# A fused MLA, retention and mixture-of-experts layer on one core: tokens gathered in fp32, four unsplit weight units in 24, a ring of twelve loaded two units at a time

## The reference, cut to what matters

```python
g_sel = argmax(h @ w_group + b_group)                    # one group of 4
e_local = top_k(e_logits[g_sel] + e_bias, 2)             # two of its 8 experts
y = (silu(xb @ w1[e]) * (xb @ w3[e])) @ w2[e]            # 32 experts, w1, w3: 2048x512, w2: 512x2048
out = sum over the 2 chosen experts of e_w * y[token]
h = layer_norm(ALPHA * h + out, ln2_g, ln2_b)
```

## Time and profile before

| what | value |
|---|---|
| median of 3 runs | 2136.24 us (2135.05 to 2139.49) |
| profiled execution, its span | 2134.4 us; the page gives no other time of it |
| PE, PEld, DVE, ACT busy | 97%, 82%, 75%, 60% of the span |
| experts' weights, issues | 380 + 4 of 1024 KB, median 10.4 and 8.1 us to landing |
| read from HBM | 595.05 MB |

### The profile page before, as it was taken

The page is one execution under the profiler, slowest core; times in us unless marked ns, Lnnn a source line. Parts: engine busy times, 40 slices in busy tenths (PEclk is TensorE's granted clock), DMA queues, the critical chain, the costliest instruction groups (busy, mean ns, idle before and its releaser), DMA issues.

```text
span 2134.4 us, 30028 instructions
## 1 busy us (share of the span) xinstructions
PE 2069.4 (97%) x11452; PEld 1749.8 (82%) x11452; DVE 1592.3 (75%) x1450; ACT 1286.2 (60%) x1064; POOL 104.7 (5%) x76
## 2 busy tenths in 40 slices
PE   8999999999999999999999999999999999999986
PEld 8998888899999998887887777777777787777764
DVE  7646664453646375455669999999999999999988
ACT  5445653333333323334347888888888888888883
POOL 1000000000000000001000000000000000000010
PEclk9999999999999999999999999999999999999998
DMA  6554335655454544557777999999999999999996
GB/s 215 159 139 158 118 120 186 208 180 172 146 176 148 166 157 143 192 197 239 233 297 287 399 421 421 421 420 419 418 420 418 421 418 417 417 417 418 417 397 251
DMA packets 168608, 606.48 MB, mean 284 GB/s; under 512 B 20252, under 2 KB 32684, under 8 KB 117452
## 3 DMA queue, kind: packets, MB, share of 16 engines
q1 hardware_dynamic: 164976, 598.01, 73.9%
q0 software_dynamic: 3552, 7.37, 1.1%
HBM read 595.05 MB, written 22.04 MB: 289 GB/s over the span
## 4 chain that ended last, share of the span: by engine, by line
PE 64%; DVE 16%; issue 9%; DMA 7%; ACT 3%; DVEq 0%; POOLq 0%; POOL 0%; SPq 0%; ACTq 0%
PE ps L1991 19%; PE ps L1972 15%; DVE wl L786 11%; DMA raw<-in_w_dram 7%; PE ps L1119 5%; PE ps L1120 5%; PE ps L2349 4%; PE ps L1116 3%; ACT wh L636 2%; PE ps L2104 2%; PE ps L1141 1%; DVE yall L951 1%; PE ps L2064 1%; PE ps L1089 1%; PE ps L2077 1%
## 5 line engine op out<-in xcount | busy, mean ns | idle before, releaser
L786 DVE TENSOR_TENSOR wl<-raw,wh 128x2048 fp32r<-128x2048 f32 x347 | 780.9, 2288 | 39.7 <-ACT wh L636 38.4
L636 ACT ACTIVATE wh<-raw 128x2048 fp32r<-128x2048 f32 x347 | 661.6, 1915 | 132.8 <-DMA raw<-in_w_dram 72.6
L1548 DVE TENSOR_TENSOR wl<-raw,wh 128x2048 fp32r<-128x2048 f32 (+1 forms) x168 | 379.8, 2263 | 283.3 <-ACT wh L1350 283.3
L1350 ACT ACTIVATE wh<-raw 128x2048 fp32r<-128x2048 f32 (+1 forms) x168 | 317.9, 1895 | 444.6 <-DMA raw<-in_w_in_dram 264.7
L1119 PE MATMUL ps<-wh,xg 128*128 128x512 f32 x896 | 373.1, 416 | 25.0 <-DVE wl L786 24.5
L1120 PE MATMUL ps<-wl,xg 128*128 128x512 f32 x880 | 345.2, 392 | 0.0
L1972 PE MATMUL ps<-hth,wh 128*128 128x272 f32 (+1 forms) x896 | 259.8, 290 | 3.1 <-DVE wl L1548 1.8
L1972 PE MATMUL ps<-htl,wh 128*128 128x272 f32 (+1 forms) x896 | 255.7, 285 | 0.0
L1972 PE MATMUL ps<-hth,wl 128*128 128x272 f32 (+1 forms) x896 | 255.6, 285 | 0.0
L1119 PEld LDWEIGHTS ps<-wh,xg 128*128 128x128 f32 x896 | 169.1, 189 | 77.2 <-DVE wl L786 28.3
L1119 PE MATMUL ps<-wh,hx 128*128 128x512 f32 x508 | 202.4, 398 | 3.5 <-DVE wl L786 1.9
(11 more groups left out here) (379 smaller groups left out, 3116.7 us busy)
## 6 DMA issues: line engine op xcount, KB each, us to landing
raw<-in_w_dram SPq DMA_DIRECT2D x380, 1024.0 KB, 10.4
raw<-in_w_in_dram SPq DMA_DIRECT2D x103, 1024.0 KB, 5.1
raw<-in_w_pa_dram SPq DMA_DIRECT2D x16, 1024.0 KB, 5.0
raw<-in_w_pb_dram SPq DMA_DIRECT2D x16, 1024.0 KB, 5.0
raw<-in_w_out_dram SPq DMA_DIRECT2D x16, 1024.0 KB, 5.1
raw<-in_w_ukv_dram SPq DMA_DIRECT2D x8, 1024.0 KB, 5.3
raw_e<-in_w_dram SPq DMA_DIRECT2D x4, 1024.0 KB, 8.1
yscr<-zeros SPq DMA_DIRECT2D x4, 1024.0 KB, 10.7
```

Of the source, the lines that this page charges most:

```text
L636: nc.scalar.activation(wh2[:, x % HELD, :], raw_of(turn, x), ACT.Copy).then_inc(s_wh2, 1)
L786: nc.vector.tensor_tensor(wl_of(turn, x), raw_of(turn, x), wh2[:, x % HELD, :].bitcast(F32), ALU.subtract).then_inc(s_wl2, 1)
L1350: nc.scalar.activation(wh[:, n % RING1, 0:c], raw1[:, n % RING1, 0:c], ACT.Copy).then_inc(s_wh, 1)
L1548: nc.vector.tensor_tensor(wl[:, n % RING1, 0:c], raw1[:, n % RING1, 0:c], wh[:, n % RING1, 0:c].bitcast(F32), ALU.subtract).then_inc(s_wl, 1)
```

## The change

It does six things.

- `XR = (1, 7, 13, 19)`: four whole units in 24 in place of two (and unit 0 still). Two of the four are w2 units, which multiply hx.
- The stream is kept in one fp32 tile xs, not in xh1 and xl1; PE gathers it in fp32, in four pieces a pair of eight fp32 matmuls of 128 columns. ACT rounds a piece to the high half of xg and DVE writes the low half (`gathered_rest`, new). DVE's `stream_rest` goes, and so do ACT's pieces five to eight.
- A ring of twelve places in six tiles of two; `load` moves two units, 2 MB, in runs of 16 KB per partition, after `done(x + 1 - 12)`. For w2 the rows of a partition are now four neighbours, so ACT's `copy_up` reads its bank in another order to match.
- The four zeroing transfers are issued in the load loop of the last gates (w_in, w_pb), and POOL's memset of zeros moves ahead of them.
- At the end the stream is added back in fp32 (`xn`), four matmuls a token tile in place of eight fp32r ones.
- DVE's loop over pairs has two pairs in its body.

```diff
-RING2 = 8
+RING2 = 12
+LOAD2 = 2
-        XR = (10, 22)
+        XR = (1, 7, 13, 19)
-        xh1 = place("xh1", [P, TT, KD, P], 98304, F32R)
-        xl1 = place("xl1", [P, TT, KD, P], 114688, F32R)
+        xs = place("xs", [P, TT, KD, P], 98304)
-        G_AT = (4, 6, 8, 10, 16, 18, 20, 22)
-        G_FIRST = (8, 9, 10, 11, 16, 18, 20, 22)
+        GQ = 4
+        G_AT = (4, 8, 16, 20)
+        G_FIRST = (8, 10, 16, 20)
...
+                if n is None or n >= RING2:
+                    done(sp, turn, x + LOAD2 - 1 - RING2)
+                elif n < 4:
+                    sp.wait_ge(s_ob, 2 * RET_PAIRS + 1)
+                elif n < 8:
+                    sp.wait_ge(s_wused, N_UNITS)
+                elif n < 10:
+                    sp.wait_ge(s_lgt, 1)
                 else:
-                    done(sp, turn, x - RING2)
+                    sp.wait_ge(s_xs, TT)
+                sp.dma_start(to, src).then_inc(s_raw2[x % RING2 // LOAD2], 16)
...
-                for c in range(KF):
-                    load(turn, x + c, w2[bass.ds(e, 1), P * c:P * (c + 1), :].rearrange("a p n -> p (a n)"))
+                v = w2[bass.ds(e, 1), :, :].rearrange("a (p c) n -> p (a c) n", p=P)
+                for c in (0, 2):
+                    load(turn, x + c, raw2[(x + c) % RING2 // 2][:, :, :], v[:, c:c + 2, :])
...
-                nc.scalar.activation(ab[:, v, :], ps[:, v, :], ACT.Copy).then_inc((s_ac, s_bc)[v], 1)
+                nc.scalar.activation(ab[:, v, :].rearrange("q (c p) -> q c p", c=KF),
+                                     ps[:, v, :].rearrange("q (p c) -> q c p", c=KF),
+                                     ACT.Copy).then_inc((s_ac, s_bc)[v], 1)
...
+            def gathered_rest(g, par, q, bank=None):
+
+                dve.wait_ge(s_xg, GQ * g + q + 1)
+                k = slice(4 * q, 4 * q + 4)
+                nc.vector.tensor_tensor(xg[:, par, k, :, SLOTS:2 * SLOTS],
+                                        ps[:, bank or 7 - q % 2, :].rearrange("p (k a s) -> p k a s", k=4, a=2),
+                                        xg[:, par, k, :, 0:SLOTS].bitcast(F32), ALU.subtract).then_inc(s_xgl, 1)
...
+            def gather_blocks(q, bank):
+
+                for b in range(4):
+                    for t in range(TT):
+                        m = nc.tensor.matmul(ps[:, bank, P * b:P * (b + 1)], xs[:, t, 4 * q + b, :], pg[:, t, :],
+                                             start=t == 0, stop=t == 1, skip_group_check=True)
                 m.then_inc(s_gt, 1)
```

More of the change, by code:

```diff
@@ L383, in moe_trunk @@
         s_nx = sem("s_nx")
[L384 to L385 removed]
+        s_raw2 = [sem(f"s_raw2_{i}") for i in range(RING2 // LOAD2)]
         s_wh2 = sem("s_wh2")
@@ L488, in sync_experts, with load @@
         def sync_experts(sp):
-            def load(turn, x, src):
+            def load(turn, x, to, src):
                 n = unit_no(turn, x)
[L492 to L500, removed]
-                else:
-                    done(sp, turn, x - RING2)
-                to = raw_of(turn, x)
-                sp.dma_start(to.rearrange("p (k n) -> p k n", k=4) if len(src.shape) == 3 else to,
-                             src).then_inc(s_early[n] if aside(turn, x) else s_raw2[slot2(turn, x)], 16)
@@ L516, in up @@
+                sp.dma_start(to, src).then_inc(s_raw2[x % RING2 // LOAD2], 16)
+            def up(turn, x, w, e):
                 v = w[bass.ds(e, 1), :, :].rearrange("a (p k) n -> p (a k) n", p=P)
-                for u in part:
-                    load(turn, x + u, v[:, 4 * u:4 * u + 4, :])
+                for u in (0, 2):
+                    to = raw2[(x + u) % RING2 // 2]
+                    load(turn, x + u, to[:, :, :].rearrange("p s (k n) -> p (s k) n", k=4), v[:, 4 * u:4 * u + 8, :])
@@ L528, in pair @@
                     down(turn, 0, 2 * p - 1)
[L529 to L536, removed]
+                up(turn, 4, w3, 2 * p)
+                up(turn, 8, w1, 2 * p + 1)
                 if last:
@@ L714, in one_round @@
                 if not early:
-                    for q in range(8):
+                    for q in range(GQ):
                         gathered(turn, 0, q)
@@ L952, in output_rest, with pair @@
                                                ALU.add).then_inc(s_ye[par], 1)
-            def pair(turn, p, first=False, early=None, last=False):
+            def pair(turn, p, par, first=False, early=None, last=False):
                 for x in body(first):
@@ L972, in pair @@
                         gather_matrix(turn + 1, 2 * p + 2)
+                    for q in range(GQ):
+                        if k == (G_FIRST if first else G_AT)[q] and not last:
+                            gathered_rest(turn + 1, 1 - par, q)
                     if k == 7 and not first:
@@ L982, in one_round @@
                     gather_matrix(turn, 0)
+                    for q in range(GQ):
+                        gathered_rest(turn, 0, q)
                     for x in range(HELD):
                         lo(turn, x)
-                pair(turn, 0, first=True, early=early)
+                pair(turn, 0, 0, first=True, early=early)
                 if early:
@@ L1195, in pair @@
                     if k == (14 if early else 12):
-                        mix(turn, j, 0, *([(s_hp, j), (s_stc, rounds)] if last else [(s_xg, 8 * (turn + 1) + 4)]))
+                        mix(turn, j, 0, *([(s_hp, j), (s_stc, rounds)] if last else [(s_xgl, GQ * (turn + 1) + 2)]))
                     if k == 20 and last:
```

176 lines of the change are left out of this document (65 added, 111 removed).

## The result

The changed kernel takes 2152.78 us (median of 4 runs, 2151.13 to 2153.54) against 2135.64 us before, the median of four runs beside it: ratio 1.008, 95% interval 1.0066 to 1.0095. It is slower by 17 us. The forecast was 2154.1 us.

The account below looks back on a forecast made before the run. PE was taken to bound the kernel at 31.0 us a half pair. 2134.4 + 18.2 + 2 - 3 + 0.7 = 2152.3 us; the runs' median lies 1.8 above the profiled execution, so 2154.1, range 2143 to 2169.

Parts of the forecast that it names:

- The bound: Expert stage: PE, DVE and transfers within 4% before; after the change PE alone lies above the old 30.35 us half pair.
- the sum of 31.0 us: PE's need per half pair: 10 x 1.81 + 2 x 3.43 + 3.76 + 2.28 = 31.0 us.
- 28 half pairs, +18.2: Second to thirtieth mix: PE adds 0.65 us to each half pair, no waits taken, +18.2 us; bounds +12.6 and +29.4.
- 16 KB runs at nothing: Expert loads: longer runs and the ring of twelve gain no time, as transfers have 0.65 us of room.
- Start, +2: Start of the expert stage: first unit near 1121 us, pd at 1156 to 1158.6, first mix 2 us later; bounds -3 and +5.
- In the last gates the four zeroings ... At nothing: Last gates: zeroings meet a transfer share of 0.62 and hold SP 0.6 to 4.6 us each, costing no time.
- End, -3 and +0.7: Last pair's first half -3 us, bounds -7 and +2; adding the stream back 10.3 us for 9.60, +0.7.
- What would show it: Signs: 28 half pairs in 865 to 875 us, transfer share near 0.97, DVE near 28 us, w2 unit 3.43 us.
- The chain rival: Every half pair: the order of work ACT to DVE to PE adds 0.6 us, time 2171 us; chance 0.22.

Follow-up runs that it names:

- the kernel that only loads: Changed kernel (16 KB runs, ring of twelve) with all units whole and 256 of each product's 512 columns left out; half pair 29.90 us.

## Why the prediction was right, term by term

**The bound.** Right. PE alone sets the expert stage, as the sum of 31.0 us said; it is 30.91. Whole units of w2, priced like those of w1 and w3 in the earlier trace rows, took the same 3.43 us: 2111.20 - 2107.54 less one step of 0.23, in the changed kernel's timeline of PE. With six whole units each more (of w3) added 1.62 us to its half pair.

```profile
2107.54 3.59 PE L1087 MATMUL ps<-raw,hx 128*128 128x512 f32 x8
2110.57 0.79 PE L1090 MATMUL ps<-wh,hx 128*128 128x512 f32 x1
2111.20 0.39 PE L1091 MATMUL ps<-wl,hx 128*128 128x512 f32 x1
```

In these half pairs the weight loads fill 668.15 of 865.40 us and the matmuls all of it, and PE had no room. The Trainium skill's rule to judge by weight-load share (Perfetto Trace Analysis, "Identifying the Most-Contended Engine") would give 668.15 / 865.40 = 77% here and room for more; the measurement decides against it in this kernel.

**28 half pairs, +18.2.** Measured +15.6. The mis-sized term is PE's own: 31.0 was 30.91, which is 28 x 0.09 = 2.5 us. With the other terms as they were, the two gather pieces and what follows them come to 30.91 - 18.1 - 6.86 - 2.28 = 3.67 us for my 3.76. The timeline agrees: from start to start the two pieces of a half pair take 1.78 and 1.70 us, where I had taken 1.80 for each. No waits remained, as assumed.

**16 KB runs at nothing.** Right for the time: 8 KB give the same 30.91 us. The saving in the transfers themselves is 1.7%, from 30.44 to 29.90 us, in the kernels with half of each product left out; they separate what no row of the kernel before could. My estimate by the Trainium skill's rule on packets (DMA: Bandwidth & Descriptors, "Why small descriptors are slow (HBM only)") was 0.6%, a third of it; how much of the rest belongs to the size of a load is open.

**Start, +2.** Measured +3.5 to the first mix and +4.7 to the second. The part inside the experts was right: counted from pg, PE's first unit came 4.2 us after it and pd 39.8, which with pg where it was gives 1121.1 and 1156.8 us, as forecast. The step that fell short is "In the last gates the four zeroings ... At nothing": beside a mean share of 0.62 ACT already waited 13.9 us for w_in's landings; now it waits 26.2, and the experts begin 1.6 us later. The size is uncertain: nine other kernels of the new layout have their first pg at 1117.33 to 1119.42 us, the two others of the old one at 1116.95 and 1117.68, so the two ranges overlap. Those of the wait for mrg, 2.7 us before and 4.0 to 4.9 now, do not. The other failure is one of counting: the first pair's second half also got a whole unit, and it was in no term (29.01 us against 27.40 with two whole units, 1.6 more).

**End, -3 and +0.7.** Measured -5.0 and +1.2. The cause of the first was named rightly and under-sized: 34.25 falls to 30.83 us by whole units alone, and in another kernel the half without ACT's reordering fell from 32.51 to 29.05. The granted clock of this half is 1.00 where it was 0.95, and PE's idle time in it fell from 4.94 to 1.48 us. At the end, from the first group of the stream added back to the last product, PE takes 11.38 us for 9.60; 0.8 us of that is a wait for DVE's yall, which no term had.

**What would show it.** Most of the signs came: 865.4 us, DVE at 28.0 us a half pair, the w2 unit at 3.43 us, the first unit near 1121 us less the late start, no waits for wl. One was wrong: the transfer share stayed at 1.00 and not 0.97. Where PE sets the pace the packets themselves take longer: between 1400 and 1700 us one of 16 KB lasts 614 ns on average in the kernel that only loads, 636 ns in the changed kernel and 659 ns with six whole units. So the share stays full while the rate drops.

The mechanism was right, but that the sum came out 1.3 us from the median is luck, because errors cancelled: +1.5 and +1.2 at the start against -2.6 in the pairs and -2.0 in the last pair. The chain rival fell with the missing waits. The last pair did give back 5 us, but the start cost more instead of giving back.

The version that beats both is the changed kernel with units 7 and 19 whole alone: 2129.6 us, 0.9974 of before, and 0.9977 the first time.

## What to carry to other kernels

Where several resources stand within a few per cent of each other, write down each one's need for a period with the waits taken out, and ask of every edit which of them it adds to. This change relieved DVE and ACT, made the transfers cheaper, and put 1.62 us on PE, which then set the time. What the rest of it gains together, 0.26%, shows only once the whole units are taken back to two; its parts were not measured one by one. And price the first and last period apart; an edit inside a period is in them too.

## What was new about the hardware

- A full transfer share says little: 428, 412 and 391 GB/s all stood at shares of 0.99 to 1.01, and 16 KB packets took 614, 636 and 659 ns.
- The same 12 MB of loads took 30.42 us in 1 MB loads of 8 KB runs and 29.90 us in 2 MB loads of 16 KB runs.
- A ring's lead hid a transfer bound for 660 us: 30.07 us a half pair with loads that need 30.44.
- Two copies on an idle POOL cost DVE 3.4 us each beside its wl and pd. Behind the last scatter they won 3.5 us in one half by relieving ACT and lost 7 us in the next.
